# A decoder step on one core: first gather ahead of the clearing scatter, row tiles counted in halves, norms ahead of sums

## What is computed

```python
h = layer_norm(DN_ALPHA * h + mix, lw['ln1_g'], lw['ln1_b'])
x2 = h.reshape(n * s, D_MODEL)
eidx, gw = route(x2, lw['w_router'], lw['router_bias'])          # 6 experts and weights per token
ffn = (swiglu(x2, w_s_gate, w_s_up, w_s_down)
       + routed_experts(x2, eidx, gw, w_e_gate, w_e_up, w_e_down))  # 64 experts, 3 x 1 MB of weights each
ple = jax.nn.sigmoid(h @ lw['w_ple_gate']) * (p @ lw['w_ple_proj'])
h = layer_norm(DN_ALPHA * h + ffn.reshape(n, s, D_MODEL) + ple, lw['ln2_g'], lw['ln2_b'])
```

## Time and profile before

| | us |
|---|---|
| median of 3 runs | 1305.3 (1304.9 to 1306.68) |
| the profiled execution, its own time | 1302.84 |
| span of its trace | 1301.0 |
| PE busy | 1232.8 (95%) |
| DVE busy | 493.2 (38%) |
| ACT busy | 305.7 (23%) |
| POOL busy | 160.0 (12%) |

### The profile page before, as it was taken

How to read it: one execution, slowest core, us unless ns; L and a number is a source line. 1 busy time by engine, 2 the same in 40 slices (tenths; PEclk the granted TensorE clock), 3 DMA queues, 4 the chain that set the end, 5 groups by cost and what they waited for, 6 DMA issues and landing times.

```text
span 1301.0 us, 23460 instructions
## 1 busy us (share of the span) xinstructions
PE 1232.8 (95%) x8867; PEld 983.0 (76%) x8868; DVE 493.2 (38%) x1087; ACT 305.7 (23%) x559; POOL 160.0 (12%) x227
## 2 busy tenths in 40 slices
PE   6999999999999999999996999989999999999876
PEld 6988879999999999998996666545555566666442
DVE  4455673432444233565973111211112221111138
ACT  3254453312121222225021111111111111111111
POOL 0200000000000000006153111111111121121100
PEclk9999999999999999999998999999999999999988
DMA  9312123222322331514416999999999999999975
GB/s 271 102 34 65 47 53 66 65 86 77 93 71 67 97 95 52 203 49 174 197 64 240 419 419 419 421 416 418 412 419 411 411 406 415 409 416 410 409 322 231
DMA packets 98657, 307.33 MB, mean 236 GB/s; under 512 B 11244, under 2 KB 62404, under 8 KB 72840
## 3 DMA queue, kind: packets, MB, share of 16 engines
q1 hardware_dynamic: 85332, 275.20, 55.2%
q0 software_dynamic: 12304, 28.60, 5.7%
q10 hardware_dynamic: 948, 2.50, 0.6%
HBM read 294.45 MB, written 26.94 MB: 247 GB/s over the span
## 4 chain that ended last, share of the span: by engine, by line
PE 47%; DMA 45%; DVE 5%; issue 1%; DVEq 1%; ACT 1%; POOL 1%; SPq 0%; ACTq 0%; POOLq 0%
DMA w_exp<-in_w_e_down_dram 41%; PE proj L1037 31%; PE proj L1217 4%; DMA part<-expert_rows 2%; PE proj L1346 2%; PE att L1142 1%; PE att L1104 1%; PE att L1226 1%; PE proj L1070 1%; DMA expert_rows<-xg,sidx_col 1%; PE att L1217 1%; PE att L1155 1%; PE proj L1330 1%; PE proj L1282 1%; DMA ident<-in_const_dram 0%
## 5 line engine op out<-in xcount | busy, mean ns | idle before, releaser
L1394 PE MATMUL att<-w_exp,xt 128*64 128x256 f32 x2560 | 288.8, 381 | 12.6 <-DMA w_exp<-in_w_e_up_dram 7.7
L1394 PEld LDWEIGHTS att<-w_exp,xt 128*64 128x64 f32 x2560 | 209.6, 137 | 100.8 <-issue 39.1
L1037 PE MATMUL proj<-h_hi,w_hi 128*128 128x288 f32 x768 | 171.2, 304 | 0.0
L1037 PE MATMUL proj<-h_hi,w_lo 128*128 128x288 f32 x768 | 164.1, 295 | 0.0
L1037 PE MATMUL proj<-h_lo,w_hi 128*128 128x288 f32 x768 | 164.0, 295 | 0.0
L1411 PE MATMUL proj<-w_exp,ht_e 128*64 128x512 f32 x640 | 146.1, 597 | 10.4 <-DMA w_exp<-in_w_e_down_dram 6.6
L1037 PEld LDWEIGHTS proj<-h_hi,w_hi 128*128 128x128 f32 x768 | 122.0, 189 | 16.2 <-issue 15.2
L1037 PEld LDWEIGHTS proj<-h_lo,w_hi 128*128 128x128 f32 x768 | 123.6, 189 | 0.0
L1037 PEld LDWEIGHTS proj<-h_hi,w_lo 128*128 128x128 f32 x768 | 123.5, 188 | 0.0
L460 DVE TENSOR_TENSOR w_lo<-w_raw,w_hi 128x2048 fp32r<-128x2048 f32 x33 | 75.6, 2291 | 95.1 <-ACT w_hi L450 88.1
L1411 PEld LDWEIGHTS proj<-w_exp,ht_e 128*64 128x64 f32 x640 | 50.4, 136 | 78.5 <-issue 75.4
(11 more groups left out here) (359 smaller groups left out, 1792.8 us busy)
## 6 DMA issues: line engine op xcount, KB each, us to landing
w_exp<-in_w_e_gate_dram SPq DMA_DIRECT2D x64, 1024.0 KB, 17.1
w_exp<-in_w_e_up_dram SPq DMA_DIRECT2D x64, 1024.0 KB, 17.4
w_exp<-in_w_e_down_dram SPq DMA_DIRECT2D x64, 1024.0 KB, 17.5
w_raw<-in_w_in_dram SPq DMA_DIRECT2D x21, 1024.0 KB
part<-expert_rows SPq DMA_DIRECT2D x8, 1536.0 KB, 20.8
w_raw<-in_w_in_dram SPq DMA_DIRECT2D x8, 512.0 KB
w_raw<-in_w_attn_out_dram SPq DMA_DIRECT2D x8, 512.0 KB
w_raw<-in_w_conv_out_dram SPq DMA_DIRECT2D x4, 1024.0 KB
```

What stands on the lines that cost most here:

```text
L1037: last = nc.tensor.matmul(proj[:, 2 * i + a, 0:HALF], lhs, x[:, c, a * HALF:(a + 1) * HALF], start=(c == 0 and n == 0), stop=(c == KC - 1 ...
L1394: last = nc.tensor.matmul(att[e * SLOT:(e + 1) * SLOT, m, 0:FF], xt[:, c, e * SLOT:(e + 1) * SLOT], weights[e][:, c, :], start=(c == 0), s ...
```

## The change

There are four edits.

1. POOL issues the first gather right after the waits on `routed`, `x2_out` and `x_zero`. The clearing scatter comes behind it and reads `ysb[:, 1, :]`, which POOL fills with zeros first (one MEMSET of 128 x 1024). POOL no longer waits for that scatter there; the later wait on `scattered` in `next_rows` still covers it.
2. Half h = 1 of a row tile counts on a semaphore of its own, `tile_in[t]` (the one that the input tile used before, renamed; it stands at 16 from then, so 32 means that half 1 has landed). PE starts a tile's sum when half 0 has landed and waits for half 1 only ahead of the fourth row. DVE waits for half 1 alone.
3. `N_ON_PE` goes from (2, 3, 4, 3) to (3, 3, 4, 4): PE sums one row more of tiles 0 and 3, DVE one less. PE's loop runs over rows outside and column halves inside.
4. On DVE the norm of a tile stands ahead of the next tile's `add_sum`, not behind it.

```diff
-N_ON_PE = (2, 3, 4, 3)
+N_ON_PE = (3, 3, 4, 4)
...
-                sp.dma_start(part[t][h][:, :, :], rows[:, h, 0:3, :]).then_inc(part_in[t], 16)
+                sp.dma_start(part[t][h][:, :, :], rows[:, h, 0:3, :]).then_inc((part_in, tile_in)[h][t], 16)
...
+            gather(0, 0, 1)
             k_half = half_passes(pool)
+            nc.gpsimd.memset(ysb[:, 1, :], 0.0).then_inc(x_zero, 1)
             nc.gpsimd.tensor_copy(sidx_col[1][:, :], tabs[:, bass.ds(k_half * 2 + 1, 1)]).then_inc(idx_ready, 1)
-            pool.wait_ge(idx_ready, 1)
+            pool.wait_ge(x_zero, 2)
+            pool.wait_ge(idx_ready, 2)
             pool.indirect_dma_start(out=rows_d[:, :], out_offset=bass.IndirectOffsetOnAxis(ap=sidx_col[1][:, 0:1], axis=0),
-                                    in_=xg[:, :, :].rearrange("p q c -> p (q c)"), in_offset=None, bounds_check=8 * T - 1,
+                                    in_=ysb[:, 1, :], in_offset=None, bounds_check=8 * T - 1,
                                     oob_is_err=False).then_inc(scattered, 16)
-            pool.wait_ge(scattered, 16)
-            gather(0, 0, 2)
...
-                    pe.wait_ge(part_in[t], 32)
-                    for half in range(2):
-                        for j in range(N_ON_PE[t]):
+                    pe.wait_ge(part_in[t], 16)
+                    for j in range(N_ON_PE[t]):
+                        if j == TOPK // 2:
+                            pe.wait_ge(tile_in[t], 32)
+                        for half in range(2):
                             nc.tensor.matmul(out[:, half, :], ident[:, :], part_row(t, j, half), start=(j == 0), stop=False)
...
-                dve.wait_ge(part_in[t], 32)
+                dve.wait_ge(tile_in[t], 32)
...
-            for s in range(NT + 2):
-                if s < NT and LAST_ORDER[s] < NT - 1:
-                    add_rows(LAST_ORDER[s])
-                if 1 <= s <= NT:
-                    add_sum(s - 1, LAST_ORDER[s - 1])
-                if s >= 2:
-                    last_norm(s - 2, LAST_ORDER[s - 2])
+            for s, t in enumerate(LAST_ORDER):
+                if t < NT - 1:
+                    add_rows(t)
+                if s:
+                    last_norm(s - 1, LAST_ORDER[s - 1])
+                add_sum(s, t)
+            last_norm(NT - 1, LAST_ORDER[NT - 1])
```

More of the change, by code:

```diff
@@ L217, in decoder_step @@
             "ld_x", "ld_c1", "ld_sink", "ld_conv", "ld_ck", "ld_cv"))
-        ld_xt = [sem(f"ld_xt{t}") for t in range(NT)]
+        tile_in = [sem(f"tile_in{t}") for t in range(NT)]
         w_dma = [sem(f"w_dma{i}") for i in range(2)]
@@ L489, in _ @@
             load(Step(0), w_in, COL_K)
-            sp.wait_ge(ld_xt[2], 16)
+            sp.wait_ge(tile_in[2], 16)
             wq = w_in[0][:, 0:Q_W].rearrange("(c p) (h n) -> p c h n", p=P, h=2)
@@ L768, in _ @@
         def _(act):
-            act.dma_start(x_tok[:, 0, :], xp[:, 0, :]).then_inc(ld_xt[0], 16)
+            act.dma_start(x_tok[:, 0, :], xp[:, 0, :]).then_inc(tile_in[0], 16)
             act.dma_start(ident[:, :], const1[:, 0:P]).then_inc(ld_x, 16)
             for t in range(1, NT - 1):
-                act.dma_start(x_tok[:, t, :], xp[:, t, :]).then_inc(ld_xt[t], 16)
-            act.dma_start(x_tok[0:NS, NT - 1, :], xs).then_inc(ld_xt[NT - 1], 16)
+                act.dma_start(x_tok[:, t, :], xp[:, t, :]).then_inc(tile_in[t], 16)
+            act.dma_start(x_tok[0:NS, NT - 1, :], xs).then_inc(tile_in[NT - 1], 16)
             act.wait_ge(ld_x, 16)
@@ L1049, in _ @@
             for n, (t, c) in enumerate(QUADS):
-                pe.wait_ge(ld_xt[t], 16)
+                pe.wait_ge(tile_in[t], 16)
                 if n >= 4:
```

## The result

| us | before | after |
|---|---|---|
| median of the runs side by side | 1305.99 (1304.9 to 1309.87) | 1291.53 (1290.34 to 1292.98) |
| the profiled execution, its own time | 1302.84 | 1291.53 |
| span of its trace | 1301.0 | 1289.7 |

The ratio is 0.9884, 95% interval 0.9861 to 0.9908 (on 1305.3 us: 15.1 less, 12.0 to 18.1). Two later comparisons of the same kernels gave 0.9896 and 0.9903. The forecast was 1294.0, a ratio of 0.9913, with a range from 1291.5 to 1299.0. The two profiled executions differ by 11.3 us, exactly the sum forecast; the medians differ by more.

What follows compares the result with a forecast made beforehand. The prediction took the DMA stream of weights as the bound, with idle DMA time ahead of it and DVE last at the end. Start 8.3 + end 3.0 = 11.3 us, so 1305.3 - 11.3 = 1294.0, range 1291.5 to 1299.0.

Steps and rivals of the forecast that it cites:

- The start: Gather ahead of the clearing scatter: idle DMA time before pair 2's loads shrinks, the stream moves forward by 8.3 us.
- 2 us for being the first on POOL: First gather's issue on POOL: takes the scatter's 3.03 us instead of the usual 1.0, so it lands at 699.0.
- it can't be more than 8.9: Cap on the start's gain: the 8.9 us of idle DMA time in 701 to 715, the bytes being the same.
- The end: Row sums and norms after the experts: one row, add_sum and norm leave the last landing's tail; gain 3.0 us.
- The 0.6 us set aside for tile 4's output: Last half's landing: up to 0.6 us later, 1283.5 taken, because tile 4's output (0.25 MB) falls ahead of it.
- The bound of 3.6 "without the output": Upper bound on the end's gain: 3.6 us if tile 4's output does not delay the last landing by 0.6.
- Late gather, low clock: Rival at the start: gather lands at 699.7 or later, PE's clock low; gain 6.3 + 3.0, 1296.0 us; chance 0.12.
- Behind the weights: Rival at the start: gather completes only when pair 1's 6 MB have, at 701.8; 1298.1 us; chance 0.06.
- A first call of 6 us: Skill's figure for loading a POOL function: gather would land near 703, start's gain 2.7 us; the prediction rejected it.
- PE sets the end: Rival at the end: PE's first sum runs at the lower clock; gain 8.3 + 0.5, 1296.5 us; chance 0.10.
- The start gives nothing: Rival: the idle gap is given back in the stream, PE being 96% busy; only the end gains, 1302.3; chance 0.05.
- Slower: Rival at the end: PE's clock stays low for half its work; 1307.8 us, slower by 2.5; chance 0.03.

Runs made afterwards that it cites:

- experiment 2: Only the start (edit 1, first gather ahead of the clearing scatter) against the kernel before: 1296.6 us, ratio 0.9931.
- experiment 3: Only the end (edits 2, 3 and 4; POOL as before) against the kernel before: 1302.45 us, ratio 0.9984.
- experiment 4: Only edit 4 (norm of a tile ahead of the next add_sum) against the kernel before: 1304.92 us, ratio 0.9996.
- experiment 6: Only edits 2 and 3 (halves and rows on PE, DVE's loop as before) against the kernel before: 1304.06 us, ratio 0.9987.
- experiment 7: Kernel before with the clearing scatter still first, reading zeros of ysb, and the gather not waiting for its landing: 1303.18 us, ratio 0.9979.
- experiment 1: The kernel before, unchanged, against itself: 1306.1 us, ratio 1.0003.
- experiment 9: Kernel before with 48 more unused products of 128x256 on PE ahead of turn(0), while it waits for the first gather: 1303.11 us, ratio 0.9983.
- experiment 5: The changed kernel, unchanged, measured again with more runs against the kernel before: 1292.18 us, ratio 0.9896.
- experiment 12: The changed kernel, unchanged, measured a third time against the kernel before: 1292.17 us, ratio 0.9903.
- experiment 8: Changed kernel with the second gather ahead of POOL's last product; against the kernel before: 1292.42 us, ratio 0.9903.
- experiment 10: Changed kernel with PE's last three pairs of experts written out instead of looped; against the kernel before: 1292.6 us, ratio 0.9900.
- experiment 11: As experiment 10, plus 9 unused 128x512 products on PE ahead of the up-weight wait near 1215; against the kernel before: 1293.16 us, ratio 0.9905.

## Why the prediction came out as it did

**The direction and both mechanisms were right.** PE's idle time ahead of turn(0) was 1.04 us (1 to 3 forecast), no stretch between 687 and 720 had an idle DMA, the load of pair 2 came 10.3 us earlier, 9.9 without the head start (8 to 10), the row loads started at 1237.39 (near 1237), and from the last landing it was 11.46 us (11 to 12). Experiments 2 and 3 show the two parts one at a time, and 4, 6 and 7 that none of the smaller edits would have done it.

**The time was forecast 1.4 to 3.8 us too high by the three comparisons, and both terms of the sum were mis-sized.** They explain 1.5 us of that. The failing steps are these.

- *The start, forecast 8.3, measured 9.2* (the lead of the loads at 914 and 1162 less the 0.4 that was there before). Three steps erred the same way. The gather's landing was taken as 699.0, with 2 us for being the first on POOL: its issue took 1.35 us, not 3.03, and it landed at 697.94. The 3.03 us were no price of being first either: in experiments 1, 4, 6 and 9, where the scatter is first as before, its issue took 1.08. turn(0) and gate unit 19 were taken at 4.2 us for want of a row at the upper clock; they took 3.9. And 0.6 us of idle DMA were left over; none were. The bound "it can't be more than 8.9", on which the lower end of the range stood, was wrong too, if only by 0.3. It was counted from the share of busy DMA engines. Counted from the bytes of the same rows it is 354 x 4 + 3 x 8 + 223 x 2 = 1886 KB in 14 us, which need 4.6 us at the stream's 412 GB/s: 9.4 us to be had. The row of 713 to 715 is the one that misled: its share is 0.76, but its 223 GB/s are only 0.54 of the stream. (The measured 9.2 lies between the two counts, and profiles of one kind differ by 0.5, so only the direction is sure.)
- *The end, forecast 3.0, measured 3.58.* The walk through DVE's steps was right to 0.1 us, with the root's wait of 1.67 (about 2 forecast). The 0.6 us set aside for tile 4's output lay ahead of the last landing, at most 0.4 us, and is counted there. The bound of 3.6 "without the output" is what came.

9.2 + 3.6 = 12.8 us, less up to 0.4 for the output. By their ratios, experiments 5 and 12 measured 13.6 and 12.7 us, the first comparison 15.1 (12.0 to 18.1). The sum lies in all three intervals and inside the range of the forecast (1292.5). What put the first comparison below the range is the other 2.3 us. Nothing in the traces accounts for them; its four runs of before lie from 1304.9 to 1309.87, and the later comparisons did not repeat them, so they look like scatter, but that isn't shown.

**The profiled pair agreed with the forecast by accident.** It differs by 11.3 us, and the terms as they came would give 12.8. The missing 1.5 us is the clock at one wait of PE in the last pairs. PE's timeline there, before and then after:

```profile
1225.07 3.67 PE L1394 MATMUL att<-w_exp,xt 128*64 128x256 f32 x32 [2.62 <-DMA w_exp<-in_w_e_up_dram]
```

```profile
1215.49 5.36 PE L1395 MATMUL att<-w_exp,xt 128*64 128x256 f32 x32 [2.59 <-DMA w_exp<-in_w_e_up_dram]
```

The wait is the same, the 32 products behind it are not. From the load at 1162.22 to the row loads it was 83.3 us before, and 84.8 from 1152.55 after. The lower clock there doesn't need the change: in the profiles with the scatter in front it was there in experiments 1, 4, 7 and 9 and absent in before, 3 and 6; in those with the gather in front it was there in after, 2, 5, 8 and 12, and absent in 10 (in 11 the wait was filled). Four of seven and five of six are too few to say whether the change makes it more frequent. The prediction took 2.5 us, the distance of one execution from the median, as a constant that the changed kernel would keep. The changed kernel's execution lay at its median, and before's was among the best of its kind: that distance was luck in three clock drops, at 16, 415 and 1225 us, that it happened to be spared.

**The rivals.**

- *Late gather, low clock*: no, 697.94 and 1.00.
- *Behind the weights*: the price was wrong, and the mechanism stays open. The gather landed 3.9 us ahead of the 701.8 that this rival needs. But that price took all 6 MB of pair 1 as issued ahead of the gather, and the program issues only three of the six parts there; in the changed kernel the fourth followed at 689.23, 1.0 us behind the gather. The three landed by 695.70, the gather at 697.94, and the fifth part at 702.8. With the scatter in front, the gather came behind all six parts, and in before and in experiments 1, 3, 4, 6 and 9 it landed 0.9 to 1.2 us behind the last of them (705.81 and 704.6 in before), whether it had been issued at 701.42 (4.40 us) or, as in 1, 4, 6 and 9, some 1.7 us earlier in its execution (6.1 to 7.1 us). Against the mechanism stands experiment 7, where it landed at 705.10, ahead of a part issued before it (692.03, landed 707.3). The rule of the Trainium skill that was named for this rival (DMA: Bandwidth & Descriptors, § Queues, rings and completion order) is neither confirmed nor refuted, since which bytes stand ahead in an engine isn't in the trace.
- *A first call of 6 us* (the Trainium skill, GPSIMD Engine Reference, § 2.1 Instruction dispatch): not seen; whichever indirect DMA came first, its issue took from 1.08 to 3.03 us.
- *PE sets the end*: not in the change's own profile, but in experiments 10 and 11, two of the seven profiles that have the new end; from the row loads to the end it was 51.0 and 49.9 us there, where the three profiles of the unaltered change and experiment 8 have 48.7 to 49.2. In 11 it was the rival's own condition, the first sum at the lower clock, and it cost 0.8 us, not 2.5.
- *The start gives nothing*: no; the lead was 9.2 us near 910 and still 9.2 near 1160.
- *Slower*: no; PE's clock was back at 1243.48 (12 products in 5.39 us).

**Open** stay what share of the start's 9.2 us is clock (experiment 9), what the gather's landing waits for, where the first comparison's last 2.3 us come from, and why the clock falls behind a wait of 2.5 us in one execution and not in another.

## What to carry to other kernels

A bound on what can be moved forward is better read from bytes per us against the stream's own rate than from the share of busy engines: the bound from the share was passed here. Where one engine issues two transfers, put the one that somebody waits for in front, ahead of the other's preparation; taking away the wait between them alone gave 2 to 3 of the start's 9 us. And before one profiled execution is used as the base of a sum, find out which of its waits were followed by the lower clock: executions of the same code differ here by 1.5 us at one such wait and by up to 3.3 at another, nearly as much as the smaller of the two terms.

## What the runs showed of the hardware

- The lower clock behind a wait of 1 to 2.6 us comes and goes between executions. Where it came, it cost this. At 16 us, 0.8 to 1.8 us on 16 products and 0.9 to 3.3 us on what stands at 415 (experiments 1, 7, 9 and 11). Behind the wait of 2.54 us at 415, another 1.5 to 1.6 us at the first load of pair 1 (1, 9 and 11); in 10 the load came no later, and there the lower clock of 522 to 528, which all others have, was missing. Near 1215 or 1225 us, 1.7 us on 32 products (5.36 against 3.67) and 1.5 at the row loads. At the fold, 1.7 us. A drop at 846 us, of the same 1.7, cost nothing: the stretch from the first load of pair 1 to the load near 1153 is as long (467.8 us) in experiment 2, which doesn't have it, as in the others.
- The first gather took 9.0 to 9.7 us in front of the scatter, with three of pair 1's six parts issued ahead of it; 10.89 us in experiment 7, 2.7 us behind a scatter in the same software queue and with all six parts ahead; and 4.40 to 7.10 us when issued near the end of those parts' transfers, where it landed 0.9 to 1.2 us behind the last of them.
